# Encoder layer with windowed attention and RG-LRU: fourth moving block and two running sums ahead of the scans, the head's gate read in step 4, first sums of weights two units later

## The reference, cut to what matters

```python
proj = x @ w_in + b_in                       # 1024 x 1024 by 1024 x 7168, then split
q, k, v, g_attn, x_rnn, g_rnn, m_attn, m_rnn = split(proj)
attn = window_attention(rope(q), rope(k), v, sink) * silu(g_attn)   # 8 heads, 2 groups, blocks of 128, |i-j| <= 128
xc   = depthwise_conv(x_rnn)                 # width 4
a, u = gates(xc)                             # two directions, 10 blocks of 128 channels
rnn  = (scan(a0, u0) + scan_reversed(a1, u1)) * silu(g_rnn)
merged = sigmoid(m_attn) * (attn @ w_branch_attn) + sigmoid(m_rnn) * (rnn @ w_branch_rnn)
x = layernorm(ALPHA * x + merged @ w_out + b_out)
```

## Time and profile before

| | us |
|---|---|
| median of 3 executions (1051.58 to 1054.05) | 1052.65 |
| the profiled execution, its own time | 1050.59 |
| its span | 1048.8 |
| TensorE busy | 1014.9 (97%) |
| VectorE / ScalarE / GpSimd busy | 686.7 / 473.1 / 617.0 |

### The profile page before, as it was taken

The page is one execution under the profiler, slowest core; times in us unless marked ns, Lnnn a source line. Parts: engine busy times, 40 slices in busy tenths (PEclk is TensorE's granted clock), DMA queues, the critical chain, the costliest instruction groups (busy, mean ns, idle before and its releaser), DMA issues. The chain is left out here.

```text
span 1048.8 us, 12973 instructions
## 1 busy us (share of the span) xinstructions
PE 1014.9 (97%) x4642; PEld 838.3 (80%) x4642; DVE 686.7 (65%) x781; ACT 473.1 (45%) x694; POOL 617.0 (59%) x374
## 2 busy tenths in 40 slices
PE   8999999999999999999979999999999999999996
PEld 6788788888888888877757888878888878888885
DVE  5746665204656653667996878868788588839755
ACT  3154445212455455474727484665746751102022
POOL 4762524455452432534587999999999834475223
PEclk9999999999999999999999999999999999999999
DMA  8343332575233211426233534344343689837012
GB/s 324 120 162 120 110 110 86 175 239 182 101 130 110 77 45 51 141 101 217 82 119 108 149 98 141 101 139 133 100 151 91 211 304 331 309 111 298 1 59 102
DMA packets 63541, 150.50 MB, mean 143 GB/s; under 512 B 6784, under 2 KB 7168, under 8 KB 63360
## 3 DMA queue, kind: packets, MB, share of 16 engines
q1 hardware_dynamic: 54848, 127.69, 36.9%
q10 hardware_dynamic: 8640, 22.11, 5.4%
HBM read 108.88 MB, written 40.89 MB: 143 GB/s over the span
## 5 line engine op out<-in xcount | busy, mean ns | idle before, releaser
L682 POOL TENSOR_SCALAR w_hi<-raw 128x1024 fp32r<-128x1024 f32 (+1 forms) x46 | 57.6, 1252 | 272.7 <-PE proj L818 218.3
L818 PE MATMUL proj<-xt_hi,w_hi 128*128 128x512 f32 x480 | 194.1, 404 | 2.3 <-DVE xt_lo L1526 1.1
L820 PE MATMUL proj<-xt_hi,w_lo 128*128 128x512 f32 x480 | 188.1, 392 | 0.0
L819 PE MATMUL proj<-xt_lo,w_hi 128*128 128x512 f32 x480 | 187.9, 391 | 0.0
L717 POOL TENSOR_TENSOR w_lo<-raw,w_hi 128x512 fp32r<-128x512 f32 x66 | 129.9, 1971 | 8.1 <-ACT w_hi L1156 3.7
L685 POOL TENSOR_TENSOR w_lo<-raw,w_hi 128x1024 fp32r<-128x1024 f32 (+1 forms) x46 | 123.4, 2682 | 3.8
L820 PEld LDWEIGHTS proj<-xt_hi,w_lo 128*128 128x128 f32 x480 | 90.2, 188 | 19.9
L818 PEld LDWEIGHTS proj<-xt_hi,w_hi 128*128 128x128 f32 x480 | 90.4, 188 | 19.0 <-DVE xt_lo L1526 2.3
L819 PEld LDWEIGHTS proj<-xt_lo,w_hi 128*128 128x128 f32 x480 | 90.5, 189 | 14.1
L1005 PE MATMUL proj<-xt_hi,w_hi 128*128 128x512 f32 x224 | 89.1, 398 | 8.3 <-DVE stage_out L1529 3.5
L1009 PE MATMUL proj<-xt_lo,w_hi 128*128 128x512 f32 x224 | 88.2, 394 | 0.0
(11 more groups left out here) (195 smaller groups left out, 2487.5 us busy)
## 6 DMA issues: line engine op xcount, KB each, us to landing
raw<-stream SPq DMA_DIRECT2D x52, 512.0 KB, 4.3
presum_a<-stream SPq DMA_DIRECT2D x42, 256.0 KB, 2.9
sums<-presum_a SPq DMA_DIRECT2D x42, 256.0 KB, 2.0
raw<-sums SPq DMA_DIRECT2D x38, 256.0 KB, 2.7
spill<-part ACTq DMA_DIRECT2D x16, 512.0 KB, 2.9
merges<-stage_out ACTq DMA_DIRECT2D x32, 256.0 KB, 2.7
raw<-stream SPq DMA_DIRECT2D x31, 256.0 KB, 2.7
raw_half<-stream SPq DMA_DIRECT2D x21, 256.0 KB, 2.7
```

Source lines behind the costliest of these rows:

```text
L682: nc.gpsimd.tensor_scalar(hi, raw[:, raw_slot, cols], 1.0, 0.0, ALU.mult, ALU.add)\
L818: begun = nc.tensor.matmul(bank, wh, mov_hi, start=first, stop=False)
L819: nc.tensor.matmul(bank, wh, mov_lo, start=False, stop=False)
L820: return begun, nc.tensor.matmul(bank, wl, mov_hi, start=False, stop=last)
```

## The change

Six things: (1) `FIRST_PRESUM` 4 in place of 2; (2) ACT reads a head's gate in step 4, not 1, and VectorE's SiLU follows in step 5, not 2; (3) in block 2 VectorE makes all of t3 before `scan_input`, and the twin sums 0 and 1 of merge twin 0 before the scans, not behind them; (4) in block 3 TensorE does product 1 of twin 1 before the gates' second half; (5) in block 9 ACT's `h_high(2)` and `(3)` go before the roots and VectorE's `h_low(2)` and `(3)` before twin sum 3; (6) SyncE issues branch unit 3 before the first two sets of parts.

```diff
--- before.py
+++ after.py
@@ -119,7 +119,7 @@
 
 
 N_SLOTS = 6
-FIRST_PRESUM = 2
+FIRST_PRESUM = 4
 
 
 BY_ACT = tuple(7 * q + i for q in MERGES[:-1] for i in (4, 5, 6))
@@ -475,7 +475,7 @@
 
 
 
-        NEXT_SCORES = 1
+        NEXT_SCORES, GATE_AT = 1, 4
         SLICES = {1: 2, 2: 2, 3: 1, 4: 2, 5: 1, 6: 2, 7: 1, 8: 2, 9: 1, 10: 2}
 
         row_bank = [t[:, h * HALF:(h + 1) * HALF] for t in (*aux, buf[1], buf[0]) for h in range(2)]
@@ -637,9 +637,9 @@
             for t, product in ((2, 1), (3, 1), (4, 3), (5, 3), (6, 4), (7, 4), (8, 4)):
                 load_h(t, product)
             load_branch(2)
+            load_branch(3)
             load_parts(0)
             load_parts(1)
-            load_branch(3)
             load_branch(4)
             load_parts(2)
             load_h(9, 4)
@@ -1061,6 +1061,8 @@
                     branch(b, 0)
                 if b >= PLAIN:
                     twin_product(merge_of(b) if twin_of(b) is None else twin_of(b), 0)
+                if b == PLAIN:
+                    twin_product(twin_of(b), 1)
                 gates(b, 1)
                 if b < 2:
                     for t in range(1, 4):
@@ -1070,7 +1072,7 @@
                 if b < PLAIN:
                     rnn_tile(("x", b + 2), 0)
                 if twin_of(b) is not None:
-                    for i in range(1, 7):
+                    for i in range(2 if b == PLAIN else 1, 7):
                         twin_product(twin_of(b), i)
                 if b >= 2:
                     for i in range(1 if b == RNN_BLOCKS - 1 else 0, 7):
@@ -1229,7 +1231,7 @@
                         last.then_inc(pt_hi_done, 1)
                     if n < NB:
                         normalize(m, n)
-                    if n == 1:
+                    if n == GATE_AT:
                         gate_evac(g, h)
                     if n == NB - 2 and first_conv:
                         pad_x(0, FILL_X0)
@@ -1461,14 +1463,14 @@
                 if last_one:
                     merge_gate(m, 1)
                     early_copy(m, 3)
+                    h_high(2)
+                    h_high(3)
                 roots(b)
                 spill_tile(b, 2)
                 spill_tile(b, 3)
                 if last_one:
                     merge_gate(m, 2)
                     merge_gate(m, 3)
-                    h_high(2)
-                    h_high(3)
                     sigmoid_of(b)
                     h_high(4)
                     h_high(5)
@@ -1635,7 +1637,7 @@
                                       pt_ps[:, i * P:(i + count) * P].rearrange("p (n c) -> p n c", c=P),
                                       pt_hi[:, at, :].bitcast(f32), ALU.subtract)
                         last.then_inc(pt_split, 1)
-                    if n == 2:
+                    if n == GATE_AT + 1:
                         silu(g, h)
                     if NB - 2 <= n <= NB and not first_conv:
                         rope(n - NB + 2, *turn)
@@ -1869,33 +1871,35 @@
                     twin_sum(q, 3)
                 if last_one:
                     twin_sum(m, 2)
-                    twin_sum(m, 3)
-                scan_input(b)
-                if last_one:
                     h_low(2)
                     h_low(3)
+                    twin_sum(m, 3)
+                if b == 2:
+                    t3_sums(0)
+                    t3_sums(1)
+                    t3_low(0)
+                    t3_low(1)
+                scan_input(b)
                 if q is not None or last_one:
                     silu_of(b)
                 if last_one:
                     h_low(4)
                     h_low(5)
                 if b == 2:
-                    for c in range(2):
-                        t3_sums(c)
-                    for c in range(2):
-                        t3_low(c)
+                    twin_sum(m, 0)
+                    twin_sum(m, 1)
                 scans(b)
                 if b == 1:
                     t_sums(0)
                     silu_gate(b)
                     t_sums(1)
-                if m is not None and not last_one:
+                if b >= PLAIN and not last_one:
                     twin_sum(m, 0)
                 gated_sum(b)
                 if b == 1:
                     t_low(0)
                     t_low(1)
-                if m is not None and not last_one:
+                if b >= PLAIN and not last_one:
                     twin_sum(m, 1)
             def gate_parts(d):
 
```

## The result

The changed kernel takes 1042.38 us (median of 4 runs, 1041.68 to 1043.64) beside 1052.41 us for the kernel before on the same chip: ratio 0.9904, 95% interval 0.9887 to 0.9921, some 10 us less. The forecast was 1047.0 with a range from 1043.1. The profiled execution of after took 1042.4 us (span 1040.6), 8.2 us less than that of before, so at this level the trace shows where four fifths of it are.

A forecast was written before the change was run, and what follows sets the result against it. TensorE, busy 97% of the span, was taken as the bound, its waits some 24 us in all. Terms -1.0 - 4.5 + 1.2 - 1.3 = -5.6 us from 1052.65 gave 1047.0 us, range 1043.1 to 1050.8.

The forecast's parts named there:

- The gate in step 4: Attention heads: moving ACT's gate read and VectorE's SiLU later gives -4.5 us net, bounds -5.7 and -1.5.
- The six waits: Heads 1 to 3 of both groups: turning of the probabilities waits for pt_lo; removing this gives 6 x 0.95 = -5.7 us.
- I take 0.2 us x 6 = 1.2 us back: Six ends of heads: the later SiLU delays q_lo past its slack, giving back 1.2 us of the gate's gain.
- the turning of step 7: Turning behind the mask of block 6: about 1 us of slack for pt_lo covers all but the upper end.
- The rival of a SiLU of 2.3 us: Heads: GpSimd's split slows SiLU to 2.3 us, turnings and q_lo come late, 1057 us in all; chance 0.05.
- First sums later: First head's gate tile: its 0.83 us wait for weights goes, with a restart; -1.0 us, bounds -0.8 and -1.1.
- that idle time hides it: Units with two parts of the sums, six for four: GpSimd's 9.91 us wait for TensorE covers the extra work.
- Block 2 to 3: Reordered t3, twin sums and early product: the hole is paid nearly as before, +1.2 us, bounds -0.2 and +3.0.
- Chain, early products, idle stretch and half clock: Block 2 to 3: ACT's and VectorE's chain sets the gates; products start earlier, TensorE idles 6 to 7 us, then 1.2 GHz.
- Branch phase: Block 9: earlier h_low(2), (3) remove TensorE's 1.6 us wait at the second branch unit; -1.3 us, bounds -1.7 and -0.8.
- the fourth unit: Fourth branch unit: TensorE, arriving earlier, may wait up to 0.6 us for h_low(7).
- From trace to median: Whole kernel: the median before lies 2.06 us above the profiled execution, so the forecast starts from 1052.65 us.

The follow-up runs named there:

- the longer SiLUs: Changed kernel with an unused sum on VectorE ahead of each SiLU, longer or half as long, result in 4 or 64 bytes: 1049.44 to 1062.64 us.
- no_block: Changed kernel with the reordering of block 2 and 3 undone, on VectorE and TensorE: 1041.74 us, ratio 0.9898 to the kernel before.
- before_again: The kernel before, unchanged, measured against itself: 1052.08 us, ratio 0.9998.
- only_sums: The kernel before with only the first sums of weights moved two units later: 1048.98 us, ratio 0.9976.
- only_branch: The kernel before with only the branch phase's edits: 1050.78 us, ratio 0.9990.
- silu_longer: Changed kernel with an unused sum over the gate's 1024 columns ahead of each SiLU, result in a new 4-byte tensor: 1062.64 us, ratio 1.0093.
- silu_half_64b: Changed kernel with an unused 0.68 us sum over 512 columns ahead of each SiLU, result in a new 64-byte tensor: 1049.44 us, ratio 0.9977.

## Why the prediction was wrong, step by step

The direction and three of four mechanisms were right, the sum was 3.3 us short by the parts (-5.6 for -8.9), and the median fell 0.7 us outside the range. Even all bounds at their best (1043.9) do not reach the measured 1042.4; the term that leaves its bounds clear of noise is that of the first sums (-1.1 at best, -2.5 measured, -1.6 to -3.5).

- **The gate in step 4.** The six waits were rightly counted (-5.7; traces: 5.7 to 5.9). The step that failed is "I take 0.2 us x 6 = 1.2 us back". I took SiLU between 1.2 and 1.6 us, q_lo 0.35 to 0.75 us late and a slack of 0.4 where the rows give 0.50; SiLU took 1.22, the mask came 0.79 us late against TensorE, the gaps behind it gave back 0.65 and not 0.5, and q_lo lost 0.14 us of 0.5. The shape was right, as the longer SiLUs show: q_lo late from 0.4 us on, the turning of step 7 beyond 1 us. Only my place on it was too far up. (Alone the part gave -6.2, 0.5 us more than the six waits, which is within its interval.) The rival of a SiLU of 2.3 us, beside which I named the Trainium skill's contention rule, did not come in the changed kernel, and that was luck in part: SiLU began 0.6 us or more ahead of GpSimd's copy in every head, and the copy was the one that got longer, 1.54 for 1.05 us. In no_block one SiLU begins 0.04 us behind a late sum of GpSimd's (169.59) instead, takes 2.34 us, and the turning behind it waits 0.49 us:

```profile
169.63 2.34 DVE L1529 SCALAR_TENSOR_TENSOR gate<-tanh_g,gate 128x1024 f32<-128x1024 f32 x1
```

- **First sums later.** The term was -1.0, and 2.5 us were measured. The first gate tile gave what was said (1.07 us). What failed is "that idle time hides it": I asked only whether GpSimd had time for two parts in a unit, not which of VectorE's operations they run beside. Two pairs in a head's second half cost 0.8 us each before, one does after; and a second gate-tile wait, absent from the one trace I had, went with them (0.57 to 1.14 us). These make 1.0 + 0.8 + 0.6 to 1.1, about the 2.5 us.
- **Block 2 to 3.** Forecast +1.2, alone +0.9 (0.0 to +1.8), and in the trace +1.9 at the gates of block 4, of which 1.0 is certain. Chain, early products, idle stretch and half clock came as written. The forecast had no place for what happens behind: a kernel that enters block 4 late gets up to 1.3 us back by block 9. In the trace of before TensorE waits 0.3 us for ACT's early copy in each of them; in every trace in which it enters block 4 late (before_again 1.2 us, only_sums 1.4, only_branch 1.4) these waits are gone, waits of 0.25 us for w_lo stand in their place, and 0.2 to 0.4 us a block come back. Why the period is shorter then is my reading of the waits, no run isolates it. If so, lateness in block 3 is half free, in the unchanged kernel too.
- **Branch phase.** Forecast -1.3, measured -1.05 alone and -1.2 in the trace. No wait opened at the fourth unit.
- **From trace to median.** I let both kernels' medians lie 2.06 us above their profiled executions. After's lies on it, so the two spans differ by 8.2 us and the two medians by 10.0. The parts' own ratios give 8.9, between the two; the rest is within the interval and stays open.

## What to carry to other kernels

When work is moved on VectorE or GpSimd, ask beside which instruction of the other each moved piece now runs and which of the two starts first, not only whether its engine has time; a pair of small sums at the wrong half of a head cost as much as the wait one was after. A chain that ends late can be filled with other work, but the time comes back only if the chain or the next engine in line (here GpSimd, idle for the gates) is moved too. Read two traces of the same kernel before trusting a wait of under 1 us or a stretch that is 1 to 2 us longer, and add no tensor to SBUF in an experiment without a run of the tensor alone.

## What the runs showed of the hardware

A tensor of four bytes in SBUF slowed most of the matmul streams. In 30 us in which TensorE waits for nothing it makes 134 matmuls in the changed kernel, 131 with the tensor of 4 bytes, 133 with 64, and 134 with 512, all at full granted clock (the second column is PE, with its count; the one behind POOL is the clock):

```profile
205.00:235.00 30.00, 30.00 (x134) 24.85 (x133) 0.00 (x0) 5.14 (x5) 16.61 (x12) 1.00 0.66 237
```

```profile
205.00:235.00 30.00, 30.00 (x131) 24.08 (x130) 0.00 (x0) 5.13 (x5) 14.66 (x11) 1.00 0.71 243
```

```profile
205.00:235.00 30.00, 30.00 (x133) 24.62 (x132) 0.00 (x0) 5.13 (x5) 16.25 (x12) 1.00 0.65 236
```

```profile
205.00:235.00 30.00, 30.00 (x134) 24.86 (x133) 0.00 (x0) 5.14 (x5) 16.44 (x12) 1.00 0.65 233
```

By start-to-start times between 200 and 235 us a 512-column matmul follows the last after 0.2267 us in the changed kernel, 0.2333 with 4 bytes (a third of them take over 0.235), 0.2288 with 64 bytes and 0.2267 with 512. Over the whole kernel the three cost +10.1, +3.2 and +0.5 us.

Two streams keep their pace. The gates' products take 0.2265 us a matmul in the changed kernel and with 4 bytes alike (0.2276 with 64), and the last product makes 377 matmuls in 85 us in both, first the changed kernel, then 4 bytes:

```profile
945.00:1030.00 85.00, 85.00 (x377) 70.38 (x376) 58.77 (x78) 13.16 (x17) 34.83 (x14) 1.00 0.24 96
```

```profile
955.00:1040.00 85.00, 85.00 (x377) 70.38 (x376) 58.24 (x78) 13.51 (x17) 34.31 (x14) 1.00 0.24 91
```

In these two both operands of a matmul (`gates_hi` and `conv_hi`, `merged` and `xt_hi`) stand behind the new tensor and move together by 32 bytes. The slowed ones multiply by `w_hi` and `w_lo`, which stay, while the other operand moves. So the distance between the two operands would explain these streams, and the moved address alone would not; this is a reading, and no run moves one operand by itself. With which step it repeats these runs do not tell. For start addresses the Trainium skill has a section on what is allowed (SBUF — State Buffer, Operand start alignment: reads by VectorE, GpSimd and DMA at element-aligned addresses were exact, and nothing was timed). It measured no matmul there, and no run here contradicts it; the price is in time alone.

In the clash of VectorE and GpSimd the one that starts second pays in these rows. at_lo (119.34) began inside a sum of GpSimd's (118.41) and took 1.78 us for 0.69. SiLU (104.60) began ahead of the copy (105.19) and stayed at 1.22, while the copy grew from 1.05 to 1.54 and ended 0.91 us behind SiLU. In silu_longer SiLU (107.40) began inside the copy and took 1.59, and GpSimd's next operation (108.00) began inside SiLU and took 3.23. Where the two start within 0.02 us of each other, as in most heads of silu_half_64b, either can be the one that pays.
